# Reordered loads before the output projection, an earlier slot for the experts' doubled blocks, and a half block left unloaded, in a one-core encoder layer with 64 experts

## What is computed

```
h = RMSNorm(x) * (1 + scale1) + shift1            # shift, scale, gate come from silu(c) @ w_ada + b_ada
q, k, v, B, C, u, g_a, g_c = split(h @ w_in)      # windowed attention over q, k, v; short convolution over C*u
x = x + gate1 * ((sigmoid(g_a)*A + sigmoid(g_c)*B_out) @ w_out)
h = RMSNorm(x) * (1 + scale2) + shift2
x = x + gate2 * HierMoE(h)                        # best of 8 groups, then the best 2 of its 8 experts
```

## Time and profile before

| what | value |
|---|---|
| median of 3 runs | 1731.87 us (1729.24 to 1745.0) |
| the profiled execution: its own time | 1740.86 us |
| its span, first to last instruction | 1739.3 us |
| mean granted TensorE clock | 0.902 of 2.4 GHz |
| DMA traffic | 485.52 MB, mean 279 GB/s |

### The profile page before, as it was taken

The page is one execution under the profiler, slowest core; times in us unless marked ns, Lnnn a source line. Parts: engine busy times, 40 slices in busy tenths (PEclk is TensorE's granted clock), DMA queues, the critical chain, the costliest instruction groups (busy, mean ns, idle before and its releaser), DMA issues.

```text
span 1739.3 us, 22002 instructions
## 1 busy us (share of the span) xinstructions
PE 1413.4 (81%) x7954; PEld 848.8 (49%) x7955; DVE 467.6 (27%) x992; ACT 241.1 (14%) x500; POOL 372.2 (21%) x583
## 2 busy tenths in 40 slices
PE   3579999999999979489898977888888877877783
PEld 2578897897898845333333333333333323323331
DVE  1524414415424424512112111112121111211113
ACT  2313222222212301101010000000000000000000
POOL 2443432433432100011111111111111111111110
PEclk9687987989887989689999999999899999999987
DMA  9443322312331261469999999999999999999994
GB/s 323 148 95 100 109 60 84 109 58 88 114 98 42 93 236 51 169 258 424 427 416 426 407 426 427 410 418 419 417 422 425 414 426 416 419 422 403 418 388 158
DMA packets 112593, 485.52 MB, mean 279 GB/s; under 512 B 15500, under 2 KB 67884, under 8 KB 87836
## 3 DMA queue, kind: packets, MB, share of 16 engines
q1 hardware_dynamic: 94832, 462.05, 65.7%
q0 software_dynamic: 13248, 13.59, 2.6%
q10 hardware_dynamic: 4492, 9.61, 1.7%
HBM read 489.47 MB, written 24.46 MB: 295 GB/s over the span
## 4 chain that ended last, share of the span: by engine, by line
PE 45%; DMA 38%; DVE 7%; ACT 4%; issue 4%; SPq 1%; ACTq 1%; POOL 0%; POOLq 0%; DVEq 0%
DMA ws<-in_w_up 30%; PE ps L924 16%; PE ps L707 13%; PE ps L936 4%; DMA ws<-in_w_down 4%; PE ps L769 3%; PE ps L800 3%; ACT arena L1080 2%; DVE arena L1277 2%; PE ps L838 2%; DMA ws<-in_w_in 2%; PE ps L787 1%; DMA arena<-arena 1%; PE ps L670 1%; DVE small L1300 1%
## 5 line engine op out<-in xcount | busy, mean ns | idle before, releaser
L924 PE MATMUL ps<-ws,arena 128*64 128x512 f32 x1920 | 464.2, 640 | 130.8 <-DMA ws<-in_w_gate 74.9
L924 PEld LDWEIGHTS ps<-ws,arena 128*64 128x64 f32 x1920 | 166.1, 147 | 427.8 <-issue 427.7
L707 PE MATMUL ps<-ws_r 128*128 128x274 f32 x1600 | 302.4, 310 | 9.7 <-issue 9.7
L707 PEld LDWEIGHTS ps<-ws_r 128*128 128x128 f32 x1600 | 252.9, 206 | 16.5 <-issue 15.1
L383 POOL TENSOR_TENSOR held<-small 128x1 f32<-128x1 f32 x226 | 45.3, 201 | 1003.0 <-DMA yc_dram<-arena,cur 300.8
L936 PE MATMUL ps<-ws,arena 128*64 128x512 f32 x960 | 212.6, 595 | 33.1 <-DMA ws<-in_w_down 26.3
L1500 DVE TENSOR_TENSOR misc<-misc,ps 128x512 f32<-128x512 f32 x33 | 22.7, 688 | 600.1 <-PE ps L924 600.1
L707 PE MATMUL ps<-arena_r,ws_r 128*128 128x274 f32 x800 | 178.0, 306 | 0.0
L936 PEld LDWEIGHTS ps<-ws,arena 128*64 128x64 f32 x960 | 75.8, 137 | 149.1 <-issue 111.0
L707 PEld LDWEIGHTS ps<-arena_r,ws_r 128*128 128x128 f32 x800 | 138.3, 206 | 0.0
L538 POOL TENSOR_TENSOR ws_r<-ws,ws_r 128x1024 fp32r<-128x1024 f32 x48 | 117.2, 2443 | 3.8
(11 more groups left out here) (266 smaller groups left out, 1239.4 us busy)
## 6 DMA issues: line engine op xcount, KB each, us to landing
ws<-in_w_gate SPq DMA_DIRECT2D x60, 2048.0 KB, 18.1
ws<-in_w_up SPq DMA_DIRECT2D x60, 2048.0 KB, 20.3
ws<-in_w_down SPq DMA_DIRECT2D x60, 2048.0 KB, 20.7
ws<-in_w_ada SPq DMA_DIRECT2D x12, 2048.0 KB, 8.8
ws<-in_w_in SPq DMA_DIRECT2D x48, 512.0 KB, 3.8
merged<-in_w_gate SPq DMA_DIRECT2D x3, 2048.0 KB, 25.2
arena<-in_w_up SPq DMA_DIRECT2D x3, 2048.0 KB, 30.1
arena<-in_w_down SPq DMA_DIRECT2D x3, 2048.0 KB, 35.0
```

What stands on the lines that cost most here:

```text
L707: last = nc.tensor.matmul(ps[:, 2 * buf + h, 0:HALF], w[:, k, :], x[:, k, HALF * h:HALF * h + HALF], start=(k == 0 and part == 0), stop=(k ...
L924: last = nc.tensor.matmul(ps[CAP * e:CAP * e + CAP, m, :], xT[c][:, k, CAP * e:CAP * e + CAP], weights[e][:, k, :], start=(k == 0), stop=( ...
```

## The change

Six edits:

1. `ORDER` becomes (0, 1, 4, 2, 3): the sample tile is third. Its mix takes the bank that the new place gives; router(0) is hooked into mix(1) instead of mix(2). ACT runs norm, store and copy of each place in turn; DVE runs place by place, with top_two(0) ahead of residual(1).
2. ACT loads x1 (4 DMAs) after the last projection, and after `merged` is complete a2bc, b2bc of the prompt and n2bc. SP loads g1bc ahead of slot 0, then waits for these four, and loads the 12 others (xq, g1q, the sample's a2bc and b2bc, both g2bc) ahead of slots 2 and 5. DVE waits for g1bc, a2bc, b2bc, n2bc and x1 before residual(0), for the rest only when the sample tile needs it.
3. The loads of double(0) go before SP's loop, after `wts_rdy`; those of double(i + 1) follow those of single(2i + 2). Before, double(i) followed single(2i + 1).
4. A new table `O_FULL` says for each single block whether its second item exists. If not, SP loads only the three even slots and raises the semaphores of the odd ones itself. PE computes both halves as before, the second with whatever the slot holds.
5. SP no longer waits for `moe_done`, which is gone, but for `y_free` of both kinds to reach the number of blocks done (from a new table entry, `O_SUM`).
6. DVE computes the new table entries before it writes `oinfo`: 2 memsets, one reduce and 3 small tensor_scalar operations.

```diff
-ORDER = (0, 4, 1, 2, 3)
+ORDER = (0, 1, 4, 2, 3)
...
@@ block.sync
+            sp.wait_ge(kcur_rdy, 2 * NJ)
+            sp.wait_ge(ada_st, 32 * NJ)
+            sp.dma_start(g1bc[:, 0, :], bass.AP(mod_dram, 2 * D, [[0, P], [1, D]])).then_inc(g1_ld, 16)
             sp.wait_ge(ada_mm, 12)
             sp.dma_start(ws[:, 0, :], mats[0][0]).then_inc(slot_ld[0], 16)
             sp.wait_ge(proj_mm, 2 + 6 * NJ)
-            sp.wait_ge(g1_ld, 16 * 5)
-            sp.wait_ge(mods_ld, 16 * 15)
+            sp.wait_ge(merged_rdy, NJ)
+            sp.wait_ge(ada_st, 32 * NJ)
+            sp.wait_ge(g1_ld, 16 * 4)
+            for q in range(4):
+                sp.dma_start(xq[32 * q:32 * q + 32, :], ...).then_inc(mods_ld, 16)
+                sp.dma_start(g1q[32 * q:32 * q + 32, :], ...).then_inc(mods_ld, 16)
+            for dst, part in ((a2bc, 4), (b2bc, 3)):
+                sp.dma_start(dst[0:DEC, 1, :], ...).then_inc(mods_ld, 16)
+            for s in range(2):
+                sp.dma_start(g2bc[:, s, :], ...).then_inc(mods_ld, 16)
             for s in (2, 5):
                 sp.dma_start(ws[:, s, :], mats[s // 2][s % 2]).then_inc(slot_ld[s], 16)
...
             def load_single(blk):
                 of = [expert(2 * blk + e) for e in range(2)]
-                for s in range(6):
-                    sp.wait_ge(slot_used[s], blk)
-                    sp.dma_start(ws[:, s, :], ...).then_inc(slot_ld[s], 16)
+                both_there = flag(blk + O_FULL)
+
+                def half_loads(halves):
+                    for s in range(6):
+                        if s % 2 in halves:
+                            sp.wait_ge(slot_used[s], blk)
+                            sp.dma_start(ws[:, s, :], ...).then_inc(slot_ld[s], 16)
+                        else:
+                            sp.sem_inc(slot_ld[s], 16)
+
+                with sp.If(both_there > 0):
+                    half_loads((0, 1))
+                with sp.If(both_there < 1):
+                    half_loads((0,))
...
+            sp.wait_ge(wts_rdy, 1)
+            doubles = flag(O_DOUB)
+            with sp.If(doubles > 0):
+                load_double(0)
             with sp.Fori(0, NBODY) as i:
                 singles = flag(i + O_SING)
                 with sp.If(singles > 0):
                     load_single(2 * i + 1)
-                doubles = flag(i + O_DOUB)
-                with sp.If(doubles > 0):
-                    load_double(i)
                 more = flag(i + O_SING + 1)
                 with sp.If(more > 0):
                     load_single(2 * i + 2)
-
-            sp.wait_ge(moe_done, 1)
+                doubles = flag(i + O_DOUB + 1)
+                with sp.If(doubles > 0):
+                    load_double(i + 1)
+
+            stored = [sp.value_load(oinfo[0:1, O_SUM + c:O_SUM + c + 1], ...) for c in range(2)]
+            for c in range(2):
+                sp.wait_ge(y_free[c], stored[c])
@@ block.gpsimd
-            hold(nc.gpsimd).then_inc(moe_done, 1)
@@ block.tensor
-            mix(1)
-            mix(2, [(6, 0)])
+            mix(1, [(6, 0)])
+            mix(2)
             mix(3, [(2, 1), (6, 2)])
             mix(4, [(6, 3)])
             router(4)
@@ block.scalar
+            act.wait_ge(proj_mm, 2 + 6 * NJ)
+            for t in range(NTT - 1):
+                act.dma_start(x1[:, t, :], x_rows[t]).then_inc(x1_ld, 16)
             act.wait_ge(ada_st, 32 * NJ)
-            act.wait_ge(proj_mm, 2 + 6 * NJ)
             act.wait_ge(merged_rdy, NJ)
-            ...
+            for dst, part in ((a2bc, 4), (b2bc, 3)):
+                act.dma_start(dst[:, 0, :], ...).then_inc(g1_ld, 16)
+            act.dma_start(n2bc, ...).then_inc(g1_ld, 16)
...
-            ...
+            for n in range(NTT):
                 norm_rows(n)
                 h2_out(n)
                 h2T_out(n)
@@ block.vector
-            dve.wait_ge(mods_ld, 16 * 15)
-            ...
-            dve.wait_ge(g1_ld, 16 * 5)
+            dve.wait_ge(g1_ld, 16 * 4)
+            ch(V.scalar_tensor_tensor(out=a2bc[:, 0, :], ...))
+            dve.wait_ge(x1_ld, 16 * 4)
             dve.wait_ge(router_ld, 16 * 11)
...
             residual(0)
             dve.wait_ge(outT_mm, 3)
             V.tensor_copy(convrow[:, :], ps[0:32, 7, 0:P]).then_inc(outT_rdy, 1)
-            ...
+            modulate(0)
+            dve.wait_ge(route_cst, 3)
+            top_two(0)
+            residual(1)
+            residual(2)
+            modulate(1)
+            top_two(1)
+            dve.wait_ge(mods_ld, 16 * 12)
+            ch(V.scalar_tensor_tensor(out=a2bc[0:DEC, 1, :], ...))
+            modulate(2)
+            top_two(2)
+            for n in (3, 4):
+                residual(n)
+                modulate(n)
+                top_two(n)
...
+            V.memset(obuf[0:1, O_DOUB + NBODY:O_DOUB + NBODY + 1], 0.0)
...
+            ch(V.tensor_reduce(obuf[0:1, O_SUM:O_SUM + 1], obuf[0:1, O_SING:O_SING + NBODY], AX.X, ALU.add))
+            V.tensor_scalar(obuf[0:1, O_SUM:O_SUM + 1], obuf[0:1, O_SUM:O_SUM + 1], 2.0, 1.0, ALU.mult, ALU.add)
+            ch(V.tensor_scalar(obuf[0:1, O_SUM + 1:O_SUM + 2], stab[0:1, 0:1], 1.0, None, ALU.add))
+            V.memset(obuf[0:1, O_FULL + NSING:O_FULL + NSING + 1], 0.0)
+            ch(V.tensor_scalar(obuf[0:1, O_FULL:O_FULL + NSING], iota64[0:1, 1:NE:2], ends[0:1, NE - 1:NE], None, ALU.is_lt))
             V.tensor_copy(oinfo[:, :], obuf[0:1, :]).then_inc(oinfo_rdy, 1)
```

More of the change, by code:

```diff
@@ L470, in _ @@
                     load_single(2 * i + 2)
-            sp.wait_ge(moe_done, 1)
+                doubles = flag(i + O_DOUB + 1)
+                with sp.If(doubles > 0):
+                    load_double(i + 1)
+            stored = [sp.value_load(oinfo[0:1, O_SUM + c:O_SUM + c + 1], min_val=1, max_val=NSING + 1) for c in range(2)]
+            for c in range(2):
+                sp.wait_ge(y_free[c], stored[c])
             for t, (_, rows, _) in enumerate(TILES):
@@ L833, in mix @@
                         for q in range(4):
-                            last = nc.tensor.matmul(ps[32 * q:32 * q + 32, 2, 0:256], merged[:, k, c0:c0 + rows],
+                            last = nc.tensor.matmul(ps[32 * q:32 * q + 32, 2 * (n % 2), 0:256], merged[:, k, c0:c0 + rows],
                                                     wo[k][:, 256 * q:256 * q + 256], start=(k == 0), stop=(k == KT8 - 1))
@@ L1099, in _ @@
                 nc.scalar.activation(halves(sga), both(0), ACT.Sigmoid).then_inc(a_free, 1)
+            act.wait_ge(proj_mm, 2 + 6 * NJ)
+            for t in range(NTT - 1):
+                act.dma_start(x1[:, t, :], x_rows[t]).then_inc(x1_ld, 16)
             act.wait_ge(ada_st, 32 * NJ)
[L1103 removed]
             act.wait_ge(merged_rdy, NJ)
[L1105 to L1118 removed]
+            for dst, part in ((a2bc, 4), (b2bc, 3)):
+                act.dma_start(dst[:, 0, :], bass.AP(mod_dram, part * D, [[0, P], [1, D]])).then_inc(g1_ld, 16)
+            act.dma_start(n2bc, bass.AP(g["norm2_w"].tensor, 0, [[0, P], [1, D]])).then_inc(g1_ld, 16)
             act.wait_ge(outT_rdy, 3)
@@ L1341, in _ @@
             ch.leave(NJ)
-            dve.wait_ge(mods_ld, 16 * 15)
-            for s in range(2):
-                n = P if s == 0 else DEC
-                ch(V.scalar_tensor_tensor(out=a2bc[0:n, s, :], in0=a2bc[0:n, s, :], scalar=1.0, in1=n2bc[0:n, :],
-                                          op0=ALU.add, op1=ALU.mult))
-            dve.wait_ge(g1_ld, 16 * 5)
+            dve.wait_ge(g1_ld, 16 * 4)
+            ch(V.scalar_tensor_tensor(out=a2bc[:, 0, :], in0=a2bc[:, 0, :], scalar=1.0, in1=n2bc, op0=ALU.add, op1=ALU.mult))
+            dve.wait_ge(x1_ld, 16 * 4)
             dve.wait_ge(router_ld, 16 * 11)
```

51 lines of the change are left out of this document (14 added, 37 removed).

## The result

The changed kernel takes 1712.36 us in the median of 4 runs (1706.57 to 1714.0), the kernel before 1735.28 us on the same chip (4 runs, 1729.24 to 1745.0): a ratio of 0.9849, 95% interval 0.9817 to 0.9881. The forecast was 1706.5 us, 25.4 less than before. The two profiled executions stand 26.8 us apart: span 1739.3 before, 1712.5 after, where 1713.9 was forecast.

A forecast was written before the change was run, and what follows sets the result against it. Slot loads were taken to pace the expert stage, TensorE to be the path in the output stage. Gains of 13.9, 1.0, 7.6 and 2.9 sum to 25.4 us: from the 1731.87 median to 1706.5, range 1699 to 1717.

The forecast's parts named there:

- front part: From the start to the first mix, 619.5 us before; no difference was forecast.
- doubles' loads: Start of expert stage: double 0 issued earlier, 12.6 us head start mostly lost to longer order and idling; gain 1.0.
- Output stage: First to last mix: earlier loads and new tile order end TensorE's wait before the third mix; gain 13.9 us.
- rival of late loads: Output stage: first tile's loads still need 21.1 us, TensorE stands 5.5 at the hook; 1712.0 us, chance 0.12.
- rival of a head start kept whole: Expert stage: TensorE never the bound behind double 2, so 12.6 us gained in place of 1.0; 1694.9 us, chance 0.07.
- slower rival: Expert stage, each block's gate loads: SP's longer program opens gaps; 1741 us at 11.5 us preparation a block, chance 0.04.
- Half block: Block 29, the last, has one item, so three of six loads go; gain 7.6 us, ends 0 and 15.4.
- End: End of run: SP itself waits for the last scatter's acknowledgement before its reload; gain 2.9 us.
- Table: Before `oinfo`: six small VectorE operations, 0.9 us more, covered by block 0's token gather; cost 0, if uncovered 0.9.

The follow-up runs named there:

- e7: Changed kernel, but SP doesn't wait for the scale, shift and gate tensors before its twelve loads and slots 2 and 5; 1711.14 us, ratio 0.9865.
- e5: Changed kernel with its new tile order, but the old loads: all 20 on ScalarE's queue, in the old order; 1724.67 us, ratio 0.9943.
- e1: Changed kernel with the doubles' loads in their old place, double i behind single 2i + 1, none ahead of the loop; 1710.55 us, ratio 0.9852.
- a0: The changed kernel once more, without any edit, as the yardstick for the runs beside it; 1715.29 us, ratio 0.9862.
- e2: Changed kernel with only double 0 loaded early, doubles 1 and 2 in their old place behind singles 3 and 5; ratio 0.9836.
- e9: Changed kernel, but SP issues double 0's loads only after block 0's gate products are done, load order kept; 1722.15 us, ratio 0.9898.
- e3: Changed kernel with both halves of every block loaded, without flag and branches in SP's single-block loads; 1718.61 us, ratio 0.9874.
- e8: Changed kernel, but SP again waits for POOL to leave its block loop before reloading the expert rows; 1719.37 us, ratio 0.9899.

## Why the prediction was right, and where not

The sum, 25.4, was near the measured 22.9 between the medians and 26.8 between the profiles, and 1712.4 lies in the range. The nearness to 26.8 is in part luck: 4.0 of it stand in the front part, for which nothing was forecast, and make up for the doubles' loads, which were forecast 4.2 too well. Term by term:

**Output stage: right.** 14.35 against 13.9, with the mechanism as told: loads in earlier, tile 0's rows ready before the hook, no idle time, 74.05 apart where 74.5 was forecast. The 0.4 over my count is what is left of two errors. The sample tile's router, which I took at a full router's 3.8 as an upper end, took 2.6 (667.16 to 669.80): its products take 1.20 (668.67) instead of 2.00, and its wait for ScalarE is 0.25 instead of 1.1. And the mixes with a hook inside took some 0.6 more in all than 13.9 each (12.18 and 1.93 around the first hook). Prediction and result stand on a small slack, 2.7 us: in e7 3.2 us later loads use it up, and in e5 loads 10 us late bring 7.24 of wait. The rival of late loads had them 8.5 later than they were (21.1 and 12.6). What the prediction did not see is that the two edits depend on each other, since it priced them as one.

**Doubles' loads: the mechanism right, the gain not there.** Forecast: 12.6 us of head start, part spent by the longer order, 8.2 idle before 989.7, a gain of 0.6 to 1. Measured: double 0 issued 2.7 ahead of block 0 (forecast 3.9, 743.7 against 747.6), block 3 5.3 us later against block 0 (106.2 and 100.9; forecast 3.0), one idle time in the place named, but 15 to 18 us long by the table, and the stage 1 to 5 us longer than in the two profiles of before. Beside e1, with the old order, a0 shows no loss (288.7 and 288.5).

The mis-sized term is the time at which TensorE frees block 6's gate slots: 247.1 (975.52 - 728.37) where I had 242.1. The queue stands still until then, so this sets the stage: block 8's gate product comes 43.8 later, where I had 44.9. The stream itself kept its pace: the 45th load landed at 235.6, forecast 233.9, in the trace's landing events. The idle time looks longer than that because a load does not land at one moment: the landing events of the 45th lie between 230.5 and 235.6. The 5.11 above is the pace to that point; to the landing it is 5.2, as forecast.

The 5.0 us are there at the end of block 5, 214.7 instead of 209.8. I had its end follow from the landing of its down pair. In the trace it follows from its up products, which start at 195.2 (923.61 - 728.37), when their weights are there; my own pace gives 192.3 for the 37th load. Then they took 9.89 instead of 7.09 (below): 2.8 us more. In a0 they took 7.09, block 5 ended at 212.4, and the stage was 2.2 us shorter. I had counted TensorE's work in waiting blocks at full speed. The rival of a head start kept whole fell with e2 and e9: 12 us are gained at the start and 15 lost behind the last double.

The slower rival, SP's longer program, fell: with the branches and without (a0, e3), with the new order and the old (a0, e1) the stage is the same within 0.3 us.

**Half block: right.** 7.76 against 7.6, and e3 gives it back (7.56). Of the 15 us of stream only that much counts, since TensorE's 23.3 remain. There were 59 gate loads, not 60.

**End: right.** 3.06 - 0.02 = 3.0 us against 2.9, by e8.

**Table: right.** The stretch that holds it is 38.4 to 38.8 in all changed kernels, 39.7 and 40.1 before: nothing was added. Why it is shorter was not looked into.

**The median.** 25.4 less than 1731.87 is 1706.5; the measured median is 5.9 above. The kernel before measured 1735.28 with the fourth run, so 3.4 of these are the level that I started from. The other 2.5 are less than either kernel's runs scatter.

## What to carry to other kernels

A stage that streams weights through a fixed set of buffers is paced by transfers plus idle time of the queue. Before moving a load ahead, count which buffers can hold what comes behind it, and where the last item of its kind leaves nothing to fetch: here an idle time of 10 to 12 us was filled, and one of about 15 us opened later. Price a wait with what follows it, since the granted clock can be low for some us afterwards (in e5 the work behind a wait of 7.24 took 4.2 us more), and test two edits of one stage singly and together: here each alone brought 1.5 and 2.8 us, both 14.35. A load that is left out at the end of such a stream is worth only what the engine behind it had been waiting for.

## What was not expected of the hardware

The granted clock in the expert stage fell to 0.50 of 2.4 GHz, the lower level of 1.2 GHz, behind some waits for weights. The changed kernel while block 3's up products start, in the columns of the earlier trace rows:

```profile
845.00:850.00 5.00, 5.00 (x12) 1.60 (x14) 0.00 (x0) 0.00 (x0) 1.55 (x4) 0.50 1.02 433
```

The 32 up matmuls of block 3, behind a wait of 3.35, took 9.95 instead of 7.09; those of block 5 (3.54) 9.89. Behind a wait of 1.65 (834.54 above) block 3's gate products took 7.09. But the length of the wait alone does not decide: in a0 block 3's up products, behind a wait of 3.36, took 7.09 too, at a granted clock of 1.00.

```profile
839.69 7.09 PE L953 MATMUL ps<-ws,arena 128*64 128x512 f32 x32 [3.36 <-DMA ws<-in_w_up]
```

What decides between the two was not found. In the stream-bound stretch that costs nothing, as the next weights aren't there yet; in block 5, where TensorE is the next bound, it went into the stage: 2.8 us in the changed kernel.
